# One norm further ahead: five PSUM banks, interleaved low parts and a later weight split at the end of attention

## The reference, cut to what matters

```python
def _diff_attention(x, w_qkv, ..., w_o, cos, sin, layer_idx):
    ...
    o = _rms_norm(o, subln, DIFF_SUBLN_EPS) * (1.0 - lam_init)
    return o.reshape(b, s, h * 2 * dh) @ w_o          # 8 heads of 128 columns

# second_block, i = 1
        h = h + y                                      # y: the attention's output
        h = h + _conv_ffn(_rms_norm(h, ffn_norm[i]), ffn_w_up[i], ffn_conv_w[i], ffn_conv_b[i], ffn_w_down[i])
```

## Time and profile before

| | |
|---|---|
| median of 3 runs | 2158.94 us (2158.81 to 2161.93) |
| the profiled execution | 2158.65 us |
| its span | 2156.8 us |
| TensorE busy | 98% of the span |
| VectorE, ScalarE, GpSimd busy | 60%, 41%, 15% |
| mean granted TensorE clock | 0.993 of full speed |

### The profile page before, as it was taken

One profiled execution on the slowest core, in us unless ns is written; L12 is line 12 of the kernel. 1 busy time (PEld: TensorE's weight loads), 2 busy tenths in 40 slices (PEclk: granted clock), 3 DMA queues, 4 the chain that ended last, 5 costly groups with the idle time before them and its releaser, 6 DMA issues.

```text
span 2156.8 us, 29470 instructions
## 1 busy us (share of the span) xinstructions
PE 2107.8 (98%) x10220; PEld 1723.7 (80%) x10220; DVE 1301.8 (60%) x1910; ACT 893.6 (41%) x1417; POOL 316.7 (15%) x243
## 2 busy tenths in 40 slices
PE   6999999999999899999999999999999999999999
PEld 4788888888888788888888888888777777888887
DVE  6877777777444554444567555634788867555422
ACT  3444344444332222232335444422566635545322
POOL 0232332232200544410110000011000000000000
PEclk8999999999999999999999999999999999999999
DMA  7333323333333344443332333333221123333322
GB/s 293 95 107 107 102 83 103 92 97 107 89 98 117 98 134 143 131 127 92 96 107 79 97 97 95 87 100 99 59 59 50 54 84 88 97 96 94 103 98 79
DMA packets 353457, 217.34 MB, mean 101 GB/s; under 512 B 7865, under 2 KB 335987, under 8 KB 351860
## 3 DMA queue, kind: packets, MB, share of 16 engines
q1 hardware_dynamic: 352579, 214.03, 33.3%
q0 software_dynamic: 288, 2.10, 0.3%
q10 hardware_dynamic: 528, 0.40, 0.1%
HBM read 212.31 MB, written 4.19 MB: 100 GB/s over the span
## 4 chain that ended last, share of the span: by engine, by line
PE 84%; DVE 9%; ACT 3%; issue 2%; DMA 1%; SPq 1%; POOL 0%; DVEq 0%; ACTq 0%; POOLq 0%
PE ps L2346 23%; PE ps L2348 23%; PE ps L2347 23%; PE ps L2522 4%; PE ps L2691 2%; PE ps L2693 2%; PE ps L2692 2%; PE ps L2373 1%; DVE small L2235 1%; DVE w_lo L1395 1%; DVE a_sb L2268 1%; DMA ada<-w_ada 1%; DVE gd_v_s L1551 1%; DVE a_t_lo L2244 1%; ACT at_swap L1287 1%
## 5 line engine op out<-in xcount | busy, mean ns | idle before, releaser
L2346 PE MATMUL ps<-h_hi,w_hi 128*128 128x512 f32 x1896 | 769.0, 406 | 7.9 <-DVE h_lo L1459 5.7
L2348 PE MATMUL ps<-h_hi,w_lo 128*128 128x512 f32 x1896 | 742.7, 392 | 0.0
L2347 PE MATMUL ps<-h_lo,w_hi 128*128 128x512 f32 x1896 | 741.4, 391 | 0.0
L1395 DVE TENSOR_TENSOR w_lo<-raw,w_hi 128x1024 fp32r<-128x1024 f32 x332 | 432.8, 1304 | 355.9 <-ACT w_hi L875 354.6
L875 ACT ACTIVATE w_hi<-raw 128x1024 fp32r<-128x1024 f32 x334 | 353.5, 1059 | 631.4 <-PE ps L2348 433.3
L2346 PEld LDWEIGHTS ps<-h_hi,w_hi 128*128 128x128 f32 x1896 | 358.2, 189 | 83.8 <-issue 17.2
L2348 PEld LDWEIGHTS ps<-h_hi,w_lo 128*128 128x128 f32 x1896 | 357.4, 188 | 77.4
L2347 PEld LDWEIGHTS ps<-h_lo,w_hi 128*128 128x128 f32 x1896 | 358.6, 189 | 65.3
L2346 PE MATMUL ps<-act_hi,w_hi 128*128 128x512 f32 x352 | 137.1, 389 | 0.0
L2348 PE MATMUL ps<-act_hi,w_lo 128*128 128x512 f32 x352 | 136.9, 389 | 0.0
L2347 PE MATMUL ps<-act_lo,w_hi 128*128 128x512 f32 x352 | 136.9, 389 | 0.0
(11 more groups left out here) (399 smaller groups left out, 2767.9 us busy)
## 6 DMA issues: line engine op xcount, KB each, us to landing
raw<-ffn_w_up SPq DMA_DIRECT2D x88, 512.0 KB, 3.7
raw<-w_in SPq DMA_DIRECT2D x72, 512.0 KB, 3.7
raw<-w_ffn_in SPq DMA_DIRECT2D x44, 512.0 KB, 5.1
raw<-ffn_w_down SPq DMA_DIRECT2D x38, 512.0 KB, 3.6
ada_w<-w_ada SPq DMA_DIRECT2D x32, 512.0 KB, 3.8
raw<-diff_w_qkv SPq DMA_DIRECT2D x24, 512.0 KB, 3.8
ada<-w_ada SPq DMA_DIRECT2D x8, 1024.0 KB, 12.4
late_w<-w_ada_f SPq DMA_DIRECT2D x16, 512.0 KB, 3.8
```

The source lines that it names most:

```text
L1395: nc.vector.tensor_tensor(w_lo[:, tile.slot], raw[:, tile.raw], w_hi[:, tile.slot].bitcast(F32), SUB)\
L2346: nc.tensor.matmul(dst, w_hi[:, tile.slot, k], hi, start=first, stop=False)
L2347: nc.tensor.matmul(dst, w_hi[:, tile.slot, k], lo, start=False, stop=False)
L2348: return nc.tensor.matmul(dst, w_lo[:, tile.slot, k], hi, start=False, stop=last)
```

## The change

Three things. The last head's projection writes its eight tiles to banks 7, 3, 4, 1, 0, 7, 3, 4. The low parts of the next norm's input stand between the additions to x, in another order than the helper's. The split of U2 goes from ahead of the additions to behind the last low part, together with U3's, and both stand ahead of the sums of squares.

```diff
-    ATT_WO = stream.stage(1, [1, 0] * 4)
+    ATT_WO = stream.stage(1, [7, 3, 4, 1, 0, 7, 3, 4])
...
-        out_used = {b: sem(f"out_used{b}") for b in (0, 1, 5, 6, 7)}
+        out_used = {b: sem(f"out_used{b}") for b in (0, 1, 3, 4, 5, 6, 7)}
...
                 else:
                     attended(7)
-                    split(Tile(after + 8))
...
-            unnormed(N_FFN1, V_FFN + KD, attended_in, (ATT_WO.tile(0, 0).ahead(),))
+            for m in range(KD):
+                attended_in(m)
+                if 1 <= m <= 4:
+                    unnormed_lo(N_FFN1, V_FFN + KD, m - 1)
+                if m >= 4:
+                    unnormed_lo(N_FFN1, V_FFN + KD, m)
+                if m == 4:
+                    add_square(N_FFN1, 1)
+            for tile in (ATT_7.tile(KD - 1, 0).ahead(), ATT_WO.tile(0, 0).ahead()):
+                split(tile)
+            for m in range(2, KD - 1):
+                add_square(N_FFN1, m)
+            mean_squares(N_FFN1)
             dve.wait_ge(rows_out, 3)
             feed_forward(2)
```

## The result

| | before | changed |
|---|---|---|
| median of 9 runs | 2160.61 us (2157.55 to 2164.88) | 2168.85 us (2167.92 to 2172.59) |
| the profiled execution: its time, span | 2158.65, 2156.8 us | 2168.85, 2167.0 us |
| mean granted TensorE clock | 0.993 | 0.989 |

The changed kernel is slower: the ratio of its time to that of before is 1.0043, 95% interval 1.0034 to 1.0052, which is 7.3 to 11.2 us; the medians are 8.2 us apart. The 9 runs of before have a median 1.7 us above that of the 3 runs that were there to predict from.

What follows compares the result with a forecast made beforehand. TensorE, busy 98% of the span, was taken to bound the kernel, with VectorE setting the end of the attention. 2158.65 + 5.9 (late start) + 2.4 (clock) = 2166.95, 2167.2 for a median; range 2164.0 to 2168.6 us.

Steps and rivals of the forecast that it cites:

- Where the chain ends: At the feed-forward's first matmul: it waits for U2's low part, now behind eight additions, eight low parts and a sum.
- The first term: At the feed-forward's start: VectorE ends U2's split at 1792.07, so the first matmul comes 5.9 us later.
- The second term: In the feed-forward's first matmuls: after over 10 us of standing TensorE starts at 1.2 GHz, costing 2.4 us.
- The upper bound of 3.4: Most the fallen clock could cost, in us: half of the longest half-level stretch, read as 26.3 to 33.1.
- What costs nothing: Around the feed-forward: later squares, the later load of the slice behind U3, U3's split and two semaphores add no time.
- The cover: At the norm's sums: squares end by 1797.0, TensorE asks at 1802.6 or later, so 5.6 us hide them.
- Sum: Whole kernel: 2158.65 + 5.9 + 2.4 = 2166.95; 0.29 below the median of the runs, so 2167.2 for a median.
- half a us each way: Margin of the range around the cases at 2164.6 and 2164.8; the range is 2164.0 to 2168.6.
- A clock that stays up: Rival at TensorE's stand: the clock doesn't fall, only the 5.9 us count, 2164.8; 13%.
- A shorter chain: Rival on VectorE: h_lo(5) to (7) find their high parts sooner, start 3.3 us late, 2164.6 with the clock's price; 6%.
- The group that opens without U2: Rival: first matmul needs no third low part, starts at 1782.4, sums wait for squares until 1797.0; 2159.2, no change; 5%.
- A late load: Rival: the slice behind U3, asked for 13.3 us later, lands behind 1811; 2169 or above; 3%.

Runs made afterwards that it cites:

- split_back: The changed kernel with U2's split back ahead of the eight additions, the rest of the change kept; ratio to before 1.0020.
- split_only: The kernel before with only U2's split moved behind the last low part, two banks and the old order kept; ratio to before 1.0027.
- uncoupled: The changed kernel with each low part from x(5) on one addition behind instead of right behind its own; ratio to before 1.0023.
- half_filled: The changed kernel with 21 extra matmuls on TensorE behind the last head's projection, into a bank nobody reads; ratio to before 1.0030.
- reordered: Kernel before with projection banks 7, 3, 4, 1, 2, 7, 3, 4, U2's split behind x(1), low parts one addition behind, squares between; ratios 0.9982, 0.9985.
- banks_only: The kernel before with the five projection banks alone, VectorE's order and U2's split as before; ratio to before 0.9990.
- clock_filled: The changed kernel with 42 extra matmuls on TensorE behind the last head's projection, into a bank nobody reads; ratio to before 1.0028.

## Why the prediction held in its mechanism and missed with its range

**Where the chain ends: right.** The wait of `product_group` for U2 held TensorE; split_back took it away and the release went back to an addition, split_only put it alone into the old kernel and made two thirds of the loss (5.94 of 8.94 us).

**The first term, 5.9 us: right.** It was 6.03. The steps through VectorE's queue put the split 14.46 us behind the last addition of heads 0 to 6, and it came at 14.50. The step from an addition to its low part is 1.47 us by the rows (1785.74 to 1787.21), as stepped, so each pair delays VectorE by the 0.87 of the text; the 0.79 in the rows is the idle time alone. Taking the three out gave 2.63 us back (uncoupled). The other 0.1 us lies between the end of the split and the first matmul, 0.36 instead of 0.26.

**The second term, 2.4 us: right in kind, mis-sized by 0.5.** It was 2.9. I took the price from one place of one trace, where the clock came back 5.1 us behind the first matmul; after the change it took 6.2 us, in uncoupled 4.9 and in split_only 4.1, with losses of 2.3 and 1.95. One execution could not size it: at that same place near the start, where all kernels are alike, the clock was back between 2.8 us (split_only) and 5.8 us (half_filled) behind the first matmul. The upper bound of 3.4 held, but its reading was wrong: the longest stretches at the half level in that trace are not the 6.8 us from 26.3, but 10.2 us each, from 36.5 to 46.7 and from 746.5 to 756.7. The Trainium skill's smaller figure per gap ("TensorE: Matmul & The Clock Gate", section "HAM oscillation — how this bites in real kernels"), 0.8 us by the estimate, is not what dense work behind a gap showed here: 1.95 to 2.94 us.

**What costs nothing: right.** The squares, the late load and U3 were hidden in the changed kernel; in split_back, where TensorE started 8 us earlier, the same order of squares was no longer hidden and brought 3.63 us of waiting and a fall of the clock. The cover, 5.6 us in the forecast and 8.7 in the trace (1798.29 to 1806.96), was there only because of the stall.

**What failed: the level in "Sum", and with it the range.** The measured 2168.85 lies 0.25 us above the upper end, 2168.6. The step that failed put the sum on the level of three runs, 2158.94, as if it were known to tenths, and gave the range "half a us each way" around its cases, 0.2 us above the 2168.4 of the forecast's own spread. The 9 runs of before have a median of 2160.61, 1.67 us higher. That alone leads out of the range: with the forecast's own terms the sum would be 2168.87. The terms do not: as measured, 6.03 and 2.94, they make 2167.9 on the old level. The nine runs were on the high side themselves; later medians of before were 2159.56 (35 runs), 2159.89 (33) and 2159.14 (23), and single runs reach from 2157.31 to 2165.02. A range of 4.6 us had no room for it. And that the medians are 8.24 us apart, where the text has 8.26, is partly luck: the traces say 8.94.

This scatter is ahead of the change's place, where all kernels of this study do the same: the last addition of heads 0 to 6 starts anywhere from 1776.19 to 1779.16. It is in the start, where the first dense matmul comes between 41.09 and 43.91, and in the way from there to the addition, 1734.01 to 1737.46 us. The granted clock has a part in both, as in the one-column matmuls above. Another place is the window from 80 to 100 us, with the wait of 3.67 us in it: its mean clock is 1.00 in before and uncoupled, 0.91 in three traces and 0.83 in the other seven. What else moves the addition was not parted.

**The rivals.** A clock that stays up: refuted (0.50 from 1786.3). A shorter chain: refuted in the changed kernel; uncoupled has one, and starts 3.4 us late where that case said 3.3. The group that opens without U2: refuted by the row that names w_lo. Its squares were sized rightly: they end 20.64 us behind the addition in the changed kernel, and it had 20.61. But it put nothing for the clock, which fell in split_back just behind a wait for the squares. A late load: refuted; the windows show the load from 1794 to 1799, and no later matmul up to 1850 has a wait in front of it.

## What to carry to other kernels

A piece of work that "only has to be done at some time" has a due time that stands in the consumer's code, here ahead of the whole group and not ahead of its third member: look for the first wait that counts it before it is moved. Of a change with several parts the one that opens buffers may be the gain and the reordering the loss; here the banks alone give 3.4 us at the place (1.8 at the end of the span) and the late split takes 5.9. Put a dependent pair (addition, high part on another engine, low part) one item apart in the queue; right behind each other each pair cost 0.9 us. And give the range of a forecast the scatter of the level that it stands on, not only that of the terms: a median of three runs was 1.7 us off here.

## What the runs showed of the hardware that was not expected

The granted clock fell to the half level behind 16 one-column matmuls (two rows of 1.05 and 1.03 us), with TensorE busy all the time, in both executions of reordered and after a wait of 0.17 us in banks_only; each time it was back some 3.4 us later, at a price of 1.6 to 1.7 us (what banks_only and reordered gain at the sums less what they gain at the end). In six traces (before, the changed kernel, clock_filled, half_filled, split_only, uncoupled) the same 16 matmuls were followed by 1.00, and with nine large matmuls between the halves it stayed at 1.00 twice. Which of the circumstances decides is open.

The time from the last matmul to the fall was not constant: 2.7 us (uncoupled), 3.2 (changed), 3.5 (split_only), 5.1 (half_filled), 4.6 at the end of the span before. A wait of 3.67 us with no fall is thus no promise that the next one of that length is free. The very same wait, 3.63 to 3.69 us in the twelve traces, had a fall in it in seven of them (in the changed kernel at 86.4, with TensorE standing until 87.9) and up to 1.2 us behind its end in three; in before and uncoupled there was none. In split_back another wait of 3.63 us, followed by the small matmuls, had the clock down 4.0 us behind its beginning.
